# A change of phase run token block by token block and column half by column half

## What is computed

```python
h = modulate(x, norm_g[l, 0], sh1, sc1)              # rms_norm(x) * g * (1 + scale) + shift
x = x + 0.5 * g1[:, None, :] * swiglu(h, w_ffn1_gu[l], w_ffn1_down[l])
h = modulate(x, norm_g[l, 1], sh2, sc2)
...                                                  # three kinds of attention into mix
x = x + g2[:, None, :] * (mix @ w_out[l])
```

## Time and profile before

| | us |
|---|---|
| median of 3 runs | 2040.48 (2038.12 to 2043.39) |
| the profiled execution | 2053.95 |
| its span in the trace | 2052.1 |

### The profile page before, as it was taken

One profiled execution on the slowest core, in us unless ns is written; L12 is line 12 of the kernel. 1 busy time (PEld: TensorE's weight loads), 2 busy tenths in 40 slices (PEclk: granted clock), 3 DMA queues, 4 the chain that ended last, 5 costly groups with the idle time before them and its releaser, 6 DMA issues.

```text
span 2052.1 us, 23660 instructions
## 1 busy us (share of the span) xinstructions
PE 1851.3 (90%) x8933; PEld 1509.5 (74%) x8933; DVE 1445.7 (70%) x1917; ACT 882.9 (43%) x1314; POOL 138.7 (7%) x264
## 2 busy tenths in 40 slices
PE   1799977889998999878899989998999899989997
PEld 0577856768887888767788878776777788867886
DVE  5677888567877788676678776566778765567444
ACT  1443335544444444555443454444333544434443
POOL 2011000001110111000011000000111000000000
PEclk9899999689999999986999999998999999999999
DMA  7789823048885898331489865344889553446552
GB/s 262 241 275 348 288 97 121 21 159 291 313 313 185 308 318 317 119 112 42 166 298 332 300 210 182 132 173 155 298 312 317 189 206 133 169 144 239 187 199 94
DMA packets 242295, 439.45 MB, mean 214 GB/s; under 512 B 16200, under 2 KB 156550, under 8 KB 241926
## 3 DMA queue, kind: packets, MB, share of 16 engines
q1 hardware_dynamic: 204810, 304.75, 44.0%
q0 software_dynamic: 36320, 131.13, 17.1%
q10 hardware_dynamic: 1052, 2.06, 0.3%
HBM read 436.79 MB, written 1.09 MB: 213 GB/s over the span
## 4 chain that ended last, share of the span: by engine, by line
PE 67%; DVE 9%; DMA 3%; ACT 3%; issue 2%; DVEq 0%; SPq 0%; ACTq 0%
PE bank L1423 20%; PE bank L1425 20%; PE bank L1424 20%; DVE weights_lo L872 3%; DMA arena<-in_w_ada 2%; PE bank L1496 2%; PE bank L1545 1%; DVE mod_acc L896 1%; DMA weights_raw<-in_w_ffn_in 1%; PE bank L1673 1%; DVE arena L1030 1%; DVE x L1032 1%; PE bank L1473 0%; PE bank L1672 0%; PE bank L1758 0%
## 5 line engine op out<-in xcount | busy, mean ns | idle before, releaser
L872 DVE TENSOR_TENSOR weights_lo<-weights_raw,weights_hi 128x1024 fp32r<-128x1024 f32 (+2 forms) x584 | 673.4, 1201 | 164.7 <-ACT weights_hi L524 164.5
L1423 PE MATMUL bank<-weights_hi,hT_hi 128*128 128x512 f32 x1760 | 698.8, 397 | 22.0 <-DVE hT_lo L1001 15.5
L1425 PE MATMUL bank<-weights_hi,hT_lo 128*128 128x512 f32 x1760 | 686.6, 390 | 0.0
L1424 PE MATMUL bank<-weights_lo,hT_hi 128*128 128x512 f32 x1760 | 686.6, 390 | 0.0
L524 ACT ACTIVATE weights_hi<-weights_raw 128x1024 fp32r<-128x1024 f32 (+2 forms) x584 | 571.3, 1037 | 133.4 <-PE bank L1425 86.6
L1423 PEld LDWEIGHTS bank<-weights_hi,hT_hi 128*128 128x128 f32 x1760 | 333.7, 190 | 97.8 <-DVE hT_lo L1001 21.6
L1425 PEld LDWEIGHTS bank<-weights_hi,hT_lo 128*128 128x128 f32 x1760 | 333.1, 189 | 70.2
L1424 PEld LDWEIGHTS bank<-weights_lo,hT_hi 128*128 128x128 f32 x1760 | 334.1, 190 | 65.4
L896 DVE SCALAR_TENSOR_TENSOR mod_acc<-arena,silu_cond,mod_acc 128x1024 f32<-128x1024 f32 x210 | 269.6, 1284 | 74.4 <-DMA arena<-in_w_mod 32.6
L606 ACT ACTIVATE actT_hi<-bank 128x512 fp32r<-128x512 f32 x66 | 39.5, 599 | 511.8 <-PE bank L1545 511.8
L1423 PE MATMUL bank<-weights_hi,actT_hi 128*128 128x512 f32 (+1 forms) x544 | 216.6, 398 | 20.6 <-DVE weights_lo L872 20.5
(11 more groups left out here) (270 smaller groups left out, 1253.0 us busy)
## 6 DMA issues: line engine op xcount, KB each, us to landing
weights_raw<-in_w_ffn_gu SPq DMA_DIRECT2D x176, 512.0 KB, 5.3
arena<-in_w_mod POOLq DMA_DIRECT2D x144, 512.0 KB, 6.3
weights_raw<-in_w_in SPq DMA_DIRECT2D x112, 512.0 KB, 4.6
arena<-in_w_ada POOLq DMA_DIRECT2D x96, 512.0 KB, 6.2
weights_raw<-in_w_ffn_down SPq DMA_DIRECT2D x88, 512.0 KB, 4.6
weights_raw<-in_w_ffn_in SPq DMA_DIRECT2D x88, 512.0 KB, 5.0
weights_raw<-in_w_ffn_out SPq DMA_DIRECT2D x44, 512.0 KB, 4.5
weights_raw<-in_w_out SPq DMA_DIRECT2D x32, 512.0 KB, 4.3
```

What stands on the lines that cost most here:

```text
L872: V.tensor_tensor(wlo[:, slot, 0:width], raw[:, slot, 0:width], whi[:, slot, 0:width].bitcast(F32), ALU.subtract).then_inc(S("lo_done"), 1)
L1423: T.matmul(o, sh, wh, start=start, stop=False)
L1424: T.matmul(o, sh, wl, start=False, stop=False)
L1425: return T.matmul(o, sl, wh, start=False, stop=stop)
```

## The change

The four steps "block t, column half h" become the unit of work.

- PE: `last_rows` does for each block and half both units, and reports each of the first three quarters (`acc_done`). `x_turn(t, banks)` transposes one block, two banks of four chunks. `first_strip` does all of block 0's part of the first strip, with `x_turn(1)` ahead of its last unit, and then block 1's. The first strip's units are reported used (`mm_done`) in block 1 only. In the first mid1 phase the bias passes stand behind the first strip and between the units of the second.
- ACT: squares of 512 columns with their own accumulators, scaled so that the sum is the mean; statistics for each block; ACT scales block 0 and the second half of block 1. `x_hi` makes the high parts of one block and four chunks. In an ffn phase two of the next phase's weight high parts stand ahead of the last silu.
- DVE: `boundary` replaces `finish_x`, `norm_stage` and the first `split_groups`: after an ffn phase all four weight low parts stand ahead of the updates, after a mid phase three, with the fourth between the steps. The scaling from PSUM works on 128 columns, sixteen instructions instead of eight.
- `x_done` counts four for each phase (`X_PARTS`). The first two modulation sums use banks 2 and 3.

```diff
-            def norm_stage(k):                                   # ACT
-                for t in range(NT):
-                    act.wait_ge(S("x_done"), NT * (k - 1) + t + 1)
-                    ins = nc.scalar.activation(xn[:, t, :], x[:, t, :], ACT.Square, accum_out=stat[:, t:t + 1])
...
+            def squares(k, t, h):
+                act.wait_ge(S("x_done"), X_PARTS * (k - 1) + 2 * t + h + 1)
+                c = slice(512 * h, 512 * (h + 1))
+                ins = nc.scalar.activation(xn[:, t, c], x[:, t, c], ACT.Square, scale=D ** -0.5, accum_out=stat[:, 2 * t + h:2 * t + h + 1])
+                if h == 1:
+                    ins.then_inc(S("ss_ready"), 1)
+            def root(k, t):
+                act.wait_ge(S("ms_ready"), 2 * (k - 1) + t + 1)
+                nc.scalar.activation(stat[:, 4 + t:5 + t], stat[:, 4 + t:5 + t], ACT.Sqrt).then_inc(S("rms_ready"), 1)
+                act.wait_ge(S("rstd_ready"), 2 * (k - 1) + t + 1)
+            def x_hi(t, h):
+                act.wait_ge(S("hf_ready"), tr[0] + 1)
+                nc.scalar.activation(hhi[:, 4 * h:4 * h + 4, P * t:P * (t + 1)], hf[:, tr[0] % 2, :].rearrange("p (k n) -> p k n", k=4),
+                                     ACT.Copy).then_inc(S("hhi_done"), 1)
+                tr[0] += 1
+            def norm_stage(k, split):
+                squares(k, 0, 0)
+                squares(k, 0, 1)
+                root(k, 0)
+                scale_x(0, 0, "xn0_ready")
+                scale_x(0, 1, "xn0_ready")
+                squares(k, 1, 0)
+                if split:
+                    x_hi(0, 0)
+                    x_hi(0, 1)
+                squares(k, 1, 1)
+                root(k, 1)
+                scale_x(1, 1, "xn1b_ready")
+                if split:
+                    x_hi(1, 0)
+                    x_hi(1, 1)
...
+                        if b == STRIPS - 1 and c + 8 < total_units:   # ACT, ffn
+                            units(c + 8, c + 10)
                         silu(b, c + 4)
                     act_hi(STRIPS - 1, n0 + UNITS_FFN - 8)
-                    prefetch(n0 + UNITS_FFN)
+                    prefetch(n0 + UNITS_FFN, 2)
...
+            def x_scaled(a, banks, t, h):                        # DVE
+                g = tr[0] + 2 * t + h
+                dve.wait_ge(S("tr_ready"), turned[0] + 2 * t + h + 1)
+                need(dve, S("hlo_done"), g - 1)
+                for i in range(4):
+                    c = 4 * h + i
+                    ins = V.tensor_scalar(hf[:, g % 2, P * i:P * (i + 1)], bank[banks[2 * t + h]][:, P * i:P * (i + 1)],
+                                          sclA[:, c:c + 1], modc[:, 8 * a["mod"] + c:8 * a["mod"] + c + 1], ALU.mult, ALU.add)
+                ins.then_inc(S("hf_ready"), 1)
...
+            def x_update(k, end, t, h):
+                if t == 1 and h == 1:
+                    dve.wait_ge(S("mm_done"), end)
+                else:
+                    dve.wait_ge(S("acc_done"), 3 * (k - 1) + 2 * t + h + 1)
+                c = slice(512 * h, 512 * (h + 1))
+                then(V.tensor_tensor(xn[:, t, c], bank[2 * t + h][:, :], gate_b[:, c], ALU.mult))
+                V.tensor_tensor(x[:, t, c], x[:, t, c], xn[:, t, c], ALU.add).then_inc(S("x_done"), 1)
+            def boundary(k, end, after, late):
+                if after is not None:
+                    for u in range(PREFETCH - late):
+                        lo_static(end + u, SLOT)
+                    scale_cols(after[2])
+                    banks = TRX_FFN if after[0] == "ffn" else TRX_MID
                 dve.wait_ge(S("gate_ready"), 16 * k)
+                x_update(k, end, 0, 0)
+                x_update(k, end, 0, 1)
+                x_stats(k + 1, 0)
+                x_update(k, end, 1, 0)
+                if after is not None:
+                    x_scaled(after[2], banks, 0, 0)
+                    x_low(0, 0)
+                    for u in range(PREFETCH - late, PREFETCH):
+                        lo_static(end + u, SLOT)
+                    x_scaled(after[2], banks, 0, 1)
+                x_update(k, end, 1, 1)
+                if after is not None:
+                    x_low(0, 1)
+                x_stats(k + 1, 1)
+                x_scale1(k + 1)
+                if after is not None:
+                    for h in range(2):
+                        x_scaled(after[2], banks, 1, h)
+                        x_low(1, h)
+                    x_split_done()
...
+            def first_strip(n, banks, trx):                      # PE
+                g0 = tr[0] - (2 if trx else 4)
+                for t in range(NT):
+                    for u in range(4):
+                        if t == 0:
+                            pe.wait_ge(S("lo_done"), n + u + 1)
+                            if u == 3 and trx:
+                                x_turn(1, trx)
+                        pe.wait_ge(S("hlo_done"), g0 + 2 * t + u // 2 + 1)
+                        for k in range(2):
+                            wh = whi[:, (n + u) % RING, 512 * k:512 * (k + 1)]
+                            wl = wlo[:, (n + u) % RING, 512 * k:512 * (k + 1)]
+                            ins = products(bank[banks[t]][:, :], 2 * u + k, t, wh, wl, u == 0 and k == 0, u == 3 and k == 1)
+                        if t == 1:
+                            ins.then_inc(S("mm_done"), 1)
```

More of the change, by code:

```diff
@@ L1130, in _ @@
                     act_lo(STRIPS - 1)
-                    finish_x(phase[0], n0 + {"ffn": UNITS_FFN, "mid1": UNITS_MID1, "mid2": UNITS_MID2}[kind])
+                    boundary(phase[0], end, after, 0 if kind == "ffn" else 1)
                 elif kind == "mid1":
```

176 lines of the change are left out of this document (94 added, 82 removed).

## The result

The changed kernel takes 2060.76 us (median of 4 runs, 2054.09 to 2062.19) against 2041.93 us for the kernel before in the same series: ratio 1.0081, 95% interval 1.0064 to 1.0099. So it is slower, by 18.8 us between the medians and 16.5 by the ratio (13 to 20). In a second series it was 2067.23 against 2043.23 us, ratio 1.0121 (1.0089 to 1.0153). The forecast had the sign, and 2060.8 lies in its range, but the size it forecast was +7.4 us, and its own narrower range, 2040 to 2056, was missed.

A forecast was written before the change was run, and what follows sets the result against it. The prediction took a chain of DVE and ACT steps at each change of phase to bound it; -3.0 + 1.5 + 5.3 + 3.2 + 0.4 = +7.4 us gave 2048 us, range 2030 to 2062 (own range 2040 to 2056).

The forecast's parts named there:

- The chain: DVE and ACT steps at each change of phase, timed from T, the start of the old phase's last product.
- After mid, -3.0: Four changes of phase after a mid phase: 48th product at T+20.1, together 80.4 instead of 83.44 us, 3.0 us gained.
- one of the forecast's two signs of being wrong: Changes of phase: wrong if the last low ends before T+15, or the granted clock is outside 0.75 to 0.9.
- After ffn, +1.5: Four of the five changes after an ffn: 48th product at T+21.0, together 84.0 against 82.5 us, 1.5 us lost.
- The bias, +5.3: Change of phase with the window's bias (T = 270.70): first reductions at about T+22.2 instead of T+16.9, 5.3 us lost.
- Nothing later takes that back: Window's bias: the 5.3 us delay stays, because DVE is the bound there for 30 us.
- The start, +3.2: First norm: DVE serves block 1 only after waiting for ACT on block 0; +3.2 us, or 0 if loads hide it.
- The end, +0.4: Last multiplication waits for the final gain's load, and that for the last add, at T+3.4 instead of T+3.0: +0.4 us.
- (C): Rival: the lower clock lasts beyond T+12 at changes of phase and PE replaces DVE in the chain; 2064 us, chance 0.15.
- (B): Rival: short instructions are cheap and the clock stays up at changes of phase; 2028 us, faster, chance 0.15.
- The loads of the modulation: POOL's loads wait for whole x, 6 us later; hidden, as first used some 25 us after T; otherwise up to 6 us each.

The follow-up runs named there:

- e4: The changed kernel with products of zeros in PE's idle time of each change of phase; 2038.12 us, ratio 0.9997 to the kernel before.
- e7: The kernel before with 22 products of zeros ahead of the transposes of each of the nine changes of phase; 2030.31 us, ratio 0.9954.
- e6: The changed kernel with four products of zeros behind the first strip of the first mid2; 2052.52 us, ratio 1.0064 to the kernel before.
- e1: The kernel before, unchanged, run again for a second profile; 2040.45 us, ratio 1.0007.
- e3: The changed kernel with block 1's update, squares, scaling and transposes moved forward, no zeros; 2077.90 us, ratio 1.0170 to the kernel before.
- e8: The changed kernel with block 1's steps moved forward and products of zeros in PE's idle time at changes of phase; 2053.40 us, ratio 1.0079 to the kernel before.
- e2_after_again: The changed kernel, unchanged, run again for a second profile; 2067.23 us, ratio 1.0121 to the kernel before.
- e10_after_no_bias: The changed kernel with the window's bias of the first mid1 left out; 2039.26 us, ratio 0.9978 to the kernel before.
- e5_before_shift: The kernel before with twelve products of zeros behind the first strip of the first mid2; 2049.24 us, ratio 1.0050.

## Why the prediction was right, and where its sizes were wrong

**The chain, right.** The forecast costed a chain of DVE and ACT steps, and the steps come where it put them: first product T+5.04 and T+6.80 (5.0, 6.8), 48th product with the clock up T+19.7 and T+20.3 (19.5, 20.2). The unit costs by form, to be read beside the earlier trace rows:

```profile
L1029 DVE TENSOR_SCALAR arena<-bank,scale_cols,mod_cols 128x128 f32<-128x128 f32 x160 | 54.6, 404 | 17.8 <-PE bank L1614 17.7
L1090 DVE TENSOR_TENSOR x<-x,arena 128x512 f32<-128x512 f32 x40 | 27.7, 692 | 1.4
L1039 DVE TENSOR_TENSOR hT_lo<-arena,hT_hi 128x512 fp32r<-128x512 f32 x40 | 27.6, 691 | 21.6 <-ACT hT_hi L562 21.6
...
L544 ACT ACTIVATE arena<-x 128x512 f32<-128x512 f32 x44 | 27.7, 630 | 45.2 <-DVE x L1090 30.9 <-DVE stat L1131 14.3
```

404 ns against 405 for the 128-wide scaling (the forecast's own rows, 538 less 143, give 395, so that the last 10 ns are chance), so halving the width saves 134 ns of 538, and four of them take 1.37 us. The idle time of L1039, 21.6 us behind ACT's high part, is overlap lost: in the old order DVE scaled the next group meanwhile. The Trainium skill (VectorE: DVE Perf Modes, section The TRN2 errata — SBUF-src ops pay a fixed extra latency per instruction) has 120 + columns cycles from PSUM, which at this width gives 0.26 us, an estimate. The trace does not agree: it has 0.404, and the measurement decides.

DVE in the same change, beside the earlier trace rows: DVE idles for ACT's statistics twice (0.79 us, and 0.19 for block 1), the update of (1,1) ends at 458.17, T+8.6 (forecast 8.7), and the last low part at T+16.9, as forecast; after ffn (T = 850.12) it ends at T+18.8 instead of 17.6, behind PE's late transposes.

```profile
449.52 0.21 DVE L1012 TENSOR_SCALAR stat<-stat 128x1 f32<-128x1 f32 x1 [0.79 <-ACT arena L544]
...
457.48 0.69 DVE L1090 TENSOR_TENSOR x<-x,arena 128x512 f32<-128x512 f32 x1
...
461.01 1.37 DVE L1029 TENSOR_SCALAR arena<-bank,scale_cols,mod_cols 128x128 f32<-128x128 f32 x4 [0.88 <-PE bank L1614]
463.08 0.69 DVE L1039 TENSOR_TENSOR hT_lo<-arena,hT_hi 128x512 fp32r<-128x512 f32 x1 [0.70 <-ACT hT_hi L562]
```

**After mid, -3.0:** -3.6 and -3.0. Right in size. But one of the forecast's two signs of being wrong came: the granted clock is 0.91, outside 0.75 to 0.9, in three of the four, since the lower level lasted only about 3.5 us there, half as long as in the earlier trace rows. In the fourth (T = 1424.03) the clock is 0.83. With the clock up in both orders the gain is 1.6 us (e4 against e7); the rest of the 3.0 to 3.6 is that the old order lost more to the lower clock.

**After ffn, +1.5:** +4.3 and +4.0. The forecast knew the term (20.2 at the full clock, 20.7 to 22.3 with the lower one) and took 21.0. PE starts block 0 at T+6.8 and its clock comes up near T+10.6 (products 0.43 us apart up to there, in the rows under e4_warm), so that eight products are slow and the second transposes 1.3 us late: 21.5 to 21.9. The lower clock lasts as long as in the earlier trace rows, as the forecast had it (0.50 from T+3.8 to T+10.6, 6.8 us, at T = 850.12). Before, most of that time passed in PE's idle time and the transposes, now it falls on products. The term was right and mis-sized: 21.0 taken, 21.5 to 21.9 measured.

**The bias, +5.3:** +9.2 and +8.7. The first reductions (292.31) come at T+22.9 instead of T+16.9, 6.0 us later; that much was foreseen. "Nothing later takes that back" was right too, but something was added: DVE, meant to be the bound, waits for PE more than before.

```profile
302.53 1.55 DVE L974 TENSOR_REDUCE window_bias<-bank 128x96 f32<-128x288 f32 x4 [0.54 <-PE bank L1575]
...
312.76 1.55 DVE L974 TENSOR_REDUCE window_bias<-bank 128x96 f32<-128x288 f32 x4 [1.68 <-PE bank L1575]
...
317.31 1.55 DVE L974 TENSOR_REDUCE window_bias<-bank 128x96 f32<-128x288 f32 x4 [0.81 <-PE bank L1575]
```

In the kernel before only the last two passes wait:

```profile
306.58 1.55 DVE L933 TENSOR_REDUCE window_bias<-bank 128x96 f32<-128x288 f32 x4 [0.80 <-PE bank L1483]
...
311.12 1.55 DVE L933 TENSOR_REDUCE window_bias<-bank 128x96 f32<-128x288 f32 x4 [0.80 <-PE bank L1483]
```

The last reductions start at T+47.9 instead of T+40.4, 7.5 us later, and the rest of the 9.2 comes behind them. From 310 to 320 PE is busy 3.70 of 10 us and its clock is 0.67, in the next 12 us it is 0.51; the kernel before holds 1.00 from 293 on. In e6, where behind the first pass DVE waits only 0.80 and 0.81 us in the last two of the same code, the 192nd product comes 5.8 us later than in e1, about the forecast.

**The start, +3.2.** DVE waits 2.63 us for block 1's squares at 36.28, and the first product starts at 68.04 instead of 65.12, +2.9. The first T varies among executions: seven of the order before average 266.3 us (264.5 to 270.7), five of the new one, without e3 and e8, 269.3 (267.5 to 271.6). So +3.0: right, and the -1.3 of the table's first column is the long execution of the kernel before.

**The end, +0.4:** +0.3 and 0.0.

**What wasn't in the sum:** the retention, +9.3, the first attention, 0 or +6.0, the second, -6.4. None of the rivals had them. (C) was right that the lower clock would cost more than forecast and came near in time (2064), but its mechanism isn't what happened: inside the changes of phase of the kernel after the clock is up by T+8.4 to T+11.2, short of the T+12 from which (C) was to decide. Its case came once in e6 (T = 1620.40: 0.50 until T+13.3, 48th product at T+23.1). (B)'s cheap instructions don't exist; its other half, a clock that stays up, is e4_warm, which gains 25 to 29 us. The loads of the modulation, costed at nothing, show no more waiting on DVE than before (31.4 us of idle time behind them against 32.6).

The step that failed is that stretches with unchanged code would keep their time. In the retention the clock fell in all four profiles of the new order without zeros (e3's variant counted) and in none of seven of the old (three of them without zeros). So here the fall goes with the new order, though e6 shows that it need not; by what it comes is open. What decides in the attention isn't settled either, since one and the same code took 85.7 and 79.7 us in the first mid1. In the second it took 79.2 to 79.5 us in five profiles of the new order and 85.6 to 86.8 in six of seven of the old, but in e3 and e8, whose order differs from the new one in the changes of phase alone, it was slow as well (the phase lasts 155.4 and 153.9 us, against 148.2 in after). So the gain there is no sure gain of the new order, and its cause is unknown.

Of the 22.8 us of the table's last column, then, 12.2 lie in the parts that the change touches (7.4 foreseen, the rest mostly the lower clock on products and the longer waits in the bias) and 10.6 in stretches that it doesn't touch.

**How much of it was luck.** The sign and the chain were reasoned and came true. That 2060.8 lies within 2030 to 2062 is in part luck: it is 1.2 us from the upper end, in the part of the range that was kept for (C), whose mechanism didn't come, and the 2067.2 of the second series lies outside. The first two profiles differ by 7.9 us, almost the 7.4 forecast, but that is chance as well, from terms of +9.2, +9.3 and -6.4 us and a long execution of the kernel before. The chance of (B) stands once as 0.15 and once as 0.14; nothing hangs on it.

## What to carry to other kernels

Starting a pipeline earlier on PE pays only as far as the last link of the chain comes earlier. Here the first product came 4.4 us earlier and the 48th half a microsecond, because the chain through DVE and ACT kept its length and lost its overlap. Before reordering such a boundary, try the cheap test first: here products of zeros in PE's idle time gave 9.5 us, and the whole reordering gave a loss. And when a small change moves the total by more than its own stretches do, lay the windows of the unchanged stretches side by side with the granted clock in view before looking for a mechanism.

## What the runs showed of the hardware

- A retention of the same 130 matmuls took 25.4 us at a granted clock of 1.00 and 34.7 at 0.70; in the new order, e3's variant counted, the clock fell there in each of the four profiles without zeros (after, e2_after_again, e3_pipe, e10_after_no_bias), in the old in none of seven (three without zeros), and in e6_after_shift, with 0.9 us of products some 70 us earlier, it did not fall. The attentions of the two mid1 phases took 79.2 to 79.8 or 84.0 to 86.8 us, the longer ones at the lower mean clock, in either kernel.
- PE kept at work through the idle time of the changes of phase held 1.00 there (e4_warm, e7_before_warm). The Trainium skill (TensorE: Matmul & The Clock Gate, section Why this matters for your kernels) advises to leave TensorE no long idle gaps between bursts of matmuls. These runs agree, with 25 to 29 us and 9.5 us.
- Twelve products of zeros, 2.7 us, lengthened the timed kernel by 9.4 us (e5_before_shift, 7 to 13 by its interval); their phase was 3.2 to 3.3 us longer, 1.0 of it ahead of them. That the surplus is the clock is likely and not shown. That a stretch of unchanged code can differ by 9.3 us with its granted clock is shown by the retention of before and after.
